# Natural channel order and a 33rd expert pair in a two-layer conv, attention and MoE step

## What is computed

```python
for i in range(2):
    sh1, sc1, g1, sh2, sc2, g2 = split(silu(c) @ ada_w[i] + ada_b[i], 6)   # per stream: c_ctx or c
    h = rms_norm(y, norm_mix[i]) * (1 + sc1) + sh1
    m = conv_module(h) if i == 0 else attention(h)
    y = y + g1 * m
    h = rms_norm(y, norm_ffn[i]) * (1 + sc2) + sh2
    y = y + g2 * (routed_experts(h) + swiglu(h, sh_w_gate[i], sh_w_up[i], sh_w_down[i]))
```

## Time and profile before

| | us |
|---|---|
| median of the 3 executions shown | 1530.44 (1530.39 to 1532.04) |
| the profiled execution's own time | 1527.38 |
| its span, first to last instruction | 1525.6 |
| TensorE busy in it | 1448.5 (95%) |
| VectorE busy | 461.9 (30%) |
| ScalarE busy | 295.8 (19%) |
| HBM traffic | 499.45 MB, mean 327 GB/s |
| mean granted TensorE clock | 0.981 |

### The profile page before, as it was taken

One profiled execution on the slowest core, in us unless ns is written; L12 is line 12 of the kernel. 1 busy time (PEld: TensorE's weight loads), 2 busy tenths in 40 slices (PEclk: granted clock), 3 DMA queues, 4 the chain that ended last, 5 costly groups with the idle time before them and its releaser, 6 DMA issues.

```text
span 1525.6 us, 23849 instructions
## 1 busy us (share of the span) xinstructions
PE 1448.5 (95%) x9543; PEld 846.7 (56%) x9543; DVE 461.9 (30%) x1450; ACT 295.8 (19%) x602; POOL 0.2 (0%) x4
## 2 busy tenths in 40 slices
PE   6899889999999999999979989999999999999995
PEld 2655686555555556555534448755555555555553
DVE  0786543222222222222233522422222222222222
ACT  2300332111111111111121312211111111111111
POOL 0000000000000000000000000000000000000000
PEclk9999989999999999999999999999999999999998
DMA  8988664699999999999941843687999999999980
GB/s 295 331 340 298 256 247 160 256 387 395 401 395 397 406 395 401 407 385 410 407 173 68 325 165 121 279 345 287 393 400 403 400 392 406 398 391 408 401 342 30
DMA packets 87792, 499.45 MB, mean 327 GB/s; under 512 B 11009, under 2 KB 27937, under 8 KB 29888
## 3 DMA queue, kind: packets, MB, share of 16 engines
q1 hardware_dynamic: 87744, 498.79, 82.1%
HBM read 497.45 MB, written 1.31 MB: 327 GB/s over the span
## 4 chain that ended last, share of the span: by engine, by line
PE 90%; DVE 3%; SPq 2%; DMA 2%; ACT 1%; issue 1%; DVEq 0%; ACTq 0%
PE ps L771 30%; PE ps L802 16%; PE ps L752 12%; PE ps L812 8%; PE ps L513 4%; PE ps L488 4%; PE ps L583 3%; PE ps L555 2%; SPq L370 2%; PE ps L708 2%; PE ps L502 1%; DMA S<-in_ada_w_dram 1%; PE ps L790 1%; PE ps L693 1%; PE ps L741 1%; PE ps L564 1%
## 5 line engine op out<-in xcount | busy, mean ns | idle before, releaser
L771 PE MATMUL ps<-ring,W 128*64 128x512 f32 x2048 | 453.4, 594 | 2.1 <-ACT W L1056 2.1
L771 PEld LDWEIGHTS ps<-ring,W 128*64 128x64 f32 x2048 | 165.9, 137 | 282.9 <-issue 277.8
L802 PE MATMUL ps<-ring,W 128*64 128x512 f32 x1024 | 233.8, 598 | 2.1 <-DVE W L1452 2.1
L752 PEld LDWEIGHTS ps<-W,hbf 128*128 128x128 bf16 x3168 | 183.0, 98 | 57.1 <-issue 52.6
L752 PE MATMUL ps<-W,hbf 128*128 128x128 bf16 x3168 | 199.1, 219 | 4.6 <-ACT W L1056 2.2
L1458 DVE TENSOR_TENSOR ypart<-ps,ypart 128x512 fp32r<-128x512 f32 x132 | 91.3, 692 | 192.7 <-ACT ypart L1067 192.7
L812 PE MATMUL ps<-comb,ypart 128*128 128x256 f32 x1056 | 142.5, 287 | 5.7 <-DVE ypart L1458 5.7
L1447 DVE SCALAR_TENSOR_TENSOR W<-W,ps 128x256 f32<-128x256 f32 x66 | 31.7, 480 | 359.4 <-ACT W L1061 359.4
L812 PEld LDWEIGHTS ps<-comb,ypart 128*128 128x128 f32 x1056 | 130.1, 189 | 10.8 <-DVE ypart L1458 9.2
L802 PEld LDWEIGHTS ps<-ring,W 128*64 128x64 f32 x1024 | 67.7, 136 | 118.8 <-issue 109.7
L1056 ACT ACTIVATE W<-ps 128x512 f32<-128x512 f32 x132 | 78.9, 598 | 279.7 <-PE ps L752 279.7
(11 more groups left out here) (195 smaller groups left out, 903.2 us busy)
## 6 DMA issues: line engine op xcount, KB each, us to landing
ring<-in_exp_w_gate_dram SPq DMA_DIRECT2D x128, 1024.0 KB, 8.8
ring<-in_exp_w_up_dram SPq DMA_DIRECT2D x128, 1024.0 KB, 10.8
ring<-in_exp_w_down_dram SPq DMA_DIRECT2D x128, 1024.0 KB, 9.7
S<-in_ada_w_dram SPq DMA_DIRECT2D x48, 1024.0 KB, 7.8
ring<-in_conv_w_dram SPq DMA_DIRECT2D x16, 512.0 KB, 7.3
S<-in_attn_wqkv_dram SPq DMA_DIRECT2D x1, 6144.0 KB, 23.1
ring<-in_conv_w_dram SPq DMA_DIRECT2D x1, 4096.0 KB, 18.3
S<-in_exp_w_gate_dram SPq DMA_DIRECT2D x4, 1024.0 KB, 11.1
```

The lines of the kernel that those rows point to most:

```text
L752: mm = pe.matmul(PG[:, kk * P:(kk + 1) * P], hbf[:, part, g, 4 * half + kk, :], gbf[:, g, :], start=(n == 0), stop=(n == 2 * 3 - 1))
L771: mm = pe.matmul(PGU[64 * b:64 * b + 64, :].rearrange("p (h f) -> p h f", h=2), xg[:, k, 64 * b:64 * b + 64], gate_up_of(w[b])[:, k], star ...
L802: mm = pe.matmul(bank[64 * b:64 * b + 64, :], hidT[:, j, 64 * b:64 * b + 64], down_of(w[b])[:, j, n * 512:(n + 1) * 512], start=(j == 0), ...
```

## The change

It has three parts. (1) Channels are in natural order throughout: chunk k holds channels 128k + p. Every step of eight in a TensorE operand goes; w1, wqkv, wo, the shared weights and the router's are loaded as "(k p) n", with rows of 2 KB, 6 KB, 4 KB, 1 KB (shared down 4 KB) and 256 bytes; w1 in four loads of 2 MB with two semaphores. Since the experts keep their order, the bf16 parts of the input are now put into it by ACT and DVE as they leave PSUM (`by_row`), while `y_parts` and `y_rest` read and write adjacent elements. (2) All small vectors (ada biases, norm gains, conv biases) come as rows of 512 bytes at the start, are transposed by TensorE with the conv taps and copied at once to one tile `vec`; eight loads must be there, not four, before that. `PE_CHUNK` is 3, not 7. (3) The first overflow pair becomes pair 32 of the pipeline, under no condition; its one-hots are built where `one_hot` of the next pair would be.

```diff
-CONV_ORDER = [0, KC - 1] + list(range(1, KC - 1))
-PE_CHUNK = KC - 1
+PE_CHUNK = 3
+CONV_ORDER = [0, PE_CHUNK] + [cc for cc in range(1, KC) if cc != PE_CHUNK]
...
-            return ypart[:, part, :, 64 - 64 * h:128 - 64 * h]
+            return ypart[:, part, 512 - 512 * h:1024 - 512 * h]
-        def by_chunk(bank):
+        def by_row(bank):
             return bank[:, :].rearrange("p (m k) -> p k m", k=KC)
...
+            sp.dma_start(crow[4 * KC:5 * KC, :], conv_b2[0].rearrange("(c p) -> c p", p=P)).then_inc(ld_rows, 16)
+            sp.dma_start(crow[5 * KC:7 * KC, :], norm_mix.rearrange("l (c p) -> (l c) p", p=P)).then_inc(ld_rows, 16)
+            sp.dma_start(crow[7 * KC:9 * KC, :], norm_ffn.rearrange("l (c p) -> (l c) p", p=P)).then_inc(ld_rows, 16)
+            sp.dma_start(arows[0:L * NADA * KC, :], ada_b.rearrange("l (c p) -> (l c) p", p=P)).then_inc(ld_rows, 16)
-            load_ada(range(2))
-            sp.dma_start(adab[:, 0], biases(0)).then_inc(ld_mod0, 16)
-            sp.dma_start(gains[:, 0, 0], cols(norm_mix[0])).then_inc(ld_mod0, 16)
-            sp.dma_start(gains[:, 0, 1], cols(norm_ffn[0])).then_inc(ld_mod0, 16)
-            load_ada(range(2, KC))
-            for cc in CONV_ORDER:
+            load_ada(range(KC))
+            for q in range(2):
                 for h in range(2):
-                    n0 = h * D + cc * P
-                    sp.dma_start(w1[:, :, n0:n0 + P],
-                                 conv_w1[0].rearrange("(p k) n -> p k n", k=KC)[:, :, n0:n0 + P]
-                                 ).then_inc(ld_w1[cc], 16)
+                    n0 = h * D + q * 512
+                    sp.dma_start(w1[:, :, n0:n0 + 512],
+                                 conv_w1[0].rearrange("(k p) n -> p k n", p=P)[:, :, n0:n0 + 512]
+                                 ).then_inc(ld_w1[q], 16)
...
                     for j in range(4):
-                        rhs = ada[:, slot, (j // 2) * D:(j // 2 + 1) * D].rearrange(
-                            "p (m q) -> p q m", q=KC)[:, 4 * (j % 2):4 * (j % 2) + 4, :]
-                        mm = pe.matmul(bank[32 * j:32 * j + 32, :].rearrange("p (q m) -> p q m", q=4),
-                                       scT[:, k, :], rhs, start=(k == 0), stop=(k == KC - 1))
+                        mm = pe.matmul(bank[32 * j:32 * j + 32, :], scT[:, k, :], ada[:, slot, j * 512:(j + 1) * 512],
+                                       start=(k == 0), stop=(k == KC - 1))
...
-                                           w[:, k, :].rearrange("p (m q) -> p q m", q=KC)[:, 2 * b + h, :],
+                                           w[:, k, (2 * b + h) * P:(2 * b + h + 1) * P],
...
-                pair(PAIRS - 1, 1, 0, N_LOOP + 2, last=True)
-                combine(PAIRS - 1, 1)
+                pair(PAIRS - 1, 1, 0, N_LOOP + 2)
+                pair(PAIRS, 0, 1, N_LOOP + 2, last=True)
+                combine(PAIRS, 0)
...
-                with pe.If(nov > 0):
-                    overflow_pair(0, 0)
-                    with pe.If(nov > 2):
-                        overflow_pair(0, 1)
+                with pe.If(nov > 2):
+                    overflow_pair(0, 1)
...
-                    act.activation(dst, ps[i][:, :], ACT.Copy).then_inc(ht_b1, 1)
+                    act.activation(hbf[:, 0, g, :, 64 * h:64 * h + 64], by_row(ps[i]), ACT.Copy).then_inc(ht_b1, 1)
...
-                        act.activation(half_of(0, h), by_chunk(bank), ACT.Copy).then_inc(act_yhi[l], 1)
+                        act.activation(half_of(0, h), bank[:, :], ACT.Copy).then_inc(act_yhi[l], 1)
...
+            dve.tensor_copy(vec[:, :], ps[7][:, 0:V_W]).then_inc(rows_in, 1)
...
+                def pair(i, par, last=False, overflow_next=False):
+                    if overflow_next:
+                        overflow_hot(PAIRS, 0)
+                    elif not last:
                         one_hot(i + 1)
...
-                pair(PAIRS - 1, 1, last=True)
+                pair(PAIRS - 1, 1, overflow_next=True)
+                pair(PAIRS, 0, last=True)
```

More of the change, by code:

```diff
@@ L204, in build_kernel @@
         crow = W[:, 3584:3712]
+        arows = W[:, 3712:3840]
         hb_f = hbf[:, :, :, :, :].rearrange("p s g k m -> p (s g k m)").bitcast(F32)
@@ L458, in overflow_pair @@
                         load_expert_at(l, e[b], 2 * (1 - half) + b, "dn")
-                with sp.If(nov > 0):
-                    overflow_pair(0, 0)
-                    with sp.If(nov > 2):
-                        overflow_pair(0, 1)
-                        with sp.If(nov > 4):
-                            with sp.Fori(1, OVF_PAIRS // 2) as it:
-                                for half in range(2):
-                                    with sp.If(nov > 4 * it + 2 * half):
-                                        overflow_pair(it, half)
+                overflow_pair(0, 0)
+                with sp.If(nov > 2):
+                    overflow_pair(0, 1)
+                    with sp.If(nov > 4):
+                        with sp.Fori(1, OVF_PAIRS // 2) as it:
+                            for half in range(2):
+                                with sp.If(nov > 4 * it + 2 * half):
+                                    overflow_pair(it, half)
                 if l == 0:
                     sp.wait_ge(pe_dn[0], 6)
-                    sp.dma_start(wqkv, attn_wqkv[0].rearrange("(p k) n -> p k n", k=KC)).then_inc(ld_qkv, 16)
+                    sp.dma_start(wqkv, attn_wqkv[0].rearrange("(k p) n -> p k n", p=P)).then_inc(ld_qkv, 16)
             for g, y in enumerate((y_prompt, y_sample)):
@@ L811, in combine @@
                         for part in range(2):
-                            pe.matmul(acc[k // 2][:, (k % 2) * TT:(k % 2 + 1) * TT], ypart[:, part, k, :],
+                            pe.matmul(acc[k // 2][:, (k % 2) * TT:(k % 2 + 1) * TT], ypart[:, part, k * P:(k + 1) * P],
                                       comb[:, par, :], start=False, stop=False, skip_group_check=True)
@@ L956, in _ @@
                         ada_copy(e, ps[e % 3])
-                    squares(dwo, 2, cv_out, lambda k: k + 1)
+                    squares(dwo, 2, cv_out, lambda k: k + 1 if k < PE_CHUNK else k)
                     for cc in range(KC):
@@ L1047, in _ @@
                     act.wait_ge(ht_r1, 4 * l + i + 1)
-                    dst = hbf[:, 1, g, 4 * h:4 * h + 4, :].rearrange("p k m -> p (k m)")
-                    act.activation(dst, ps[i][:, :], ACT.Copy).then_inc(ht_b2, 1)
+                    act.activation(hbf[:, 1, g, :, 64 * h:64 * h + 64], by_row(ps[i]), ACT.Copy).then_inc(ht_b2, 1)
                 act.wait_ge(sh_gu, l + 1)
@@ L1084, in _ @@
                         pair(2 * it + half + 3)
-                pair(PAIRS - 1, last=True)
+                pair(PAIRS - 1)
+                pair(PAIRS, last=True)
                 def overflow_pair(it, par):
@@ L1457, in y_rest, with overflow_hot @@
                         dve.wait_ge(act_yhi[l], 2 * i + 1 + h)
-                        dve.tensor_tensor(half_of(1, h), by_chunk(bank), half_of(0, h), ALU.subtract
+                        dve.tensor_tensor(half_of(1, h), bank[:, :], half_of(0, h), ALU.subtract
                                           ).then_inc(dve_ylo[l], 1)
-                def pair(i, par, last=False):
-                    if not last:
+                def overflow_hot(i, j):
+                    e = [dve.value_load(table[0:1, bass.ds(2 * j + b + 1, 1)], min_val=0, max_val=NE - 1)
+                         for b in range(2)]
+                    dve.wait_ge(dve_ov[l], 3 * j + 1)
+                    for b in range(2):
+                        dve.tensor_copy(wst[:, :, :, b:b + 1], wt3[:, :, :, bass.ds(e[b], 1)])
+                        for g in range(G):
+                            ins = dve.tensor_scalar(gbf[:, g, 64 * b:64 * b + 64], iota,
+                                                    ovrank[:, g, bass.ds(e[b], 1)], None, ALU.is_equal)
+                        if b == 0:
+                            ins.then_inc(dve_ov[l], 1)
+                            dve.wait_ge(dve_ov[l], 3 * j + 2)
+                        else:
+                            ins.then_inc(dve_g[l], 1)
+                            dve.wait_ge(dve_g[l], i + 1)
+                        dve.tensor_scalar(ovrank[:, :, :], ovrank[:, :, :], -float(SLOTS), None, ALU.add
+                                          ).then_inc(dve_ov[l], 1)
+                        dve.wait_ge(dve_ov[l], 3 * j + b + 3)
+                def pair(i, par, last=False, overflow_next=False):
+                    if overflow_next:
+                        overflow_hot(PAIRS, 0)
+                    elif not last:
                         one_hot(i + 1)
```

136 lines of the change are left out of this document (52 added, 84 removed).

## The result

| | before | after |
|---|---|---|
| median of the executions timed side by side, 4 each | 1530.41 us (1530.03 to 1532.04) | 1518.12 us (1517.27 to 1519.93) |
| the profiled execution's own time | 1527.38 | 1518.69 |
| its span | 1525.6 | 1516.9 |
| mean granted TensorE clock | 0.981 | 0.948 |

The ratio is 0.9923, with a 95% interval of 0.9911 to 0.9934: faster by 12.3 us, not by the 42.8 that I forecast. 1518.1 lies above the whole range. The change did most of what it was to do, and then TensorE ran at half its clock through most of the heads of layer 1's attention.

The account below looks back on a forecast made before the run. TensorE was taken to bound the expert loop, which the change leaves alone; gains lie at loop ends and mixers: 10.3 + 16.5 + 7.8 + 4.8 + 1.7 + 0.8 + 0.9 = 42.8 off 1530.44, giving 1487.6 us, range 1481 to 1514.

Parts of the forecast that it names:

- part 2: Ada products: adjacent columns save 0.875 us a unit; 17.1 in the conv stage, 7.8 in layer 1's attention.
- Part 3: Conv stage start: first product waits for half of w1, at 44 against 43.4 us; loss 0.6, bounds gain 2, loss 4.
- what is late next is DVE: Conv stage: DVE's last chunk could start at 133.3 instead of 153.05 us, allowing TensorE savings up to 19.8.
- The last square: Conv stage end: the last DVE chunk is squared last, so one square and its sum fewer, 0.8 us saved.
- rival B: Ada unit halves but w1's half, DVE's chain or the one-hots come late: 5 to 9 less saved, 1493 to 1497; chance 0.1.
- The tails: Expert loops' ends: the overflow pair inside the pipeline takes 30.68 instead of 35.86 us; 5.2 saved per layer, 10.3 in both.
- The halving of an ada unit: Ada products: a unit of 8 records falls from 1.87 to 1.0 us; saving 0.9, bounds 0 and 1.0.
- rival A: Ada unit stays at 1.87 us, four streams sharing what one step wasted: 18.4 saved, 1512 us; chance 0.22.
- The stationary operand: Weights no longer loaded in steps: 2.4 us saved in each of two projections, 4.8 together, and 1.7 in shared down.
- Output copies with the end: Kernel's end: four output copies go from 1121 towards 597 ns but wait for transposes; 0.9 us saved, bounds 0.5 and 2.
- Rival C: Overflow pair gains nothing, its weights late in the pipeline: 10.3 less saved, 1498 us; chance 0.03.
- Rival D: Natural-order loads of w1 and wqkv run far below their rate, at 100 GB/s: 39 us slower, 1570; chance 0.03.

Follow-up runs that it names:

- zeros ahead of the heads: Changed kernel with zero-operand products added after each of the four ada units ahead of layer 1's attention heads (32 to 35): 1493.89 us, ratio 0.9772.
- quarters: Changed kernel with w1 loaded in four column quarters (eight 1 MB loads, 1 KB rows) and TensorE's chunk put at 1: 1514.93 us, ratio 0.9905.
- quarters and zeros together: Changed kernel with w1 in four column quarters and zero-operand products after the four ada units ahead of the heads: 1492.62 us, ratio 0.9752.
- zeros between the heads: Changed kernel with zero-operand products only after ada units 36 to 39, one in each of the first four heads: 1500.28 us, ratio 0.9813.

## Why the prediction was wrong, and where it was right

**The step that failed** is in part 2, *attention of layer 1*: "10 x 0.875 = 8.75; DVE and ACT between heads would show about 1 of it: 7.8". It counted units at the full clock and took for granted that the rest of the stage kept the clock it had. None of the rivals was this: the prediction took the clock of every stage as given, though the stage table shows it for each. In its place the runs show a loss of 22.1: the clock costs 24.3 (143.75 against 119.5 with zeros ahead of the heads), and what remains beside it is a gain of 2.1, not 7.8. In that run the part from the first head on took 59.69 instead of the 63.51 of before, 3.8 less: the ten units took 12.0 instead of 19.6, and lower clock toward the end, in two stretches between 860 and 881, gave half of that back (its line 660, which is line 642 of the changed kernel, took 3.61 there for sixteen records and 1.93 at the full clock). From the gain of 3.8 goes 1.7 for the qkv product, 36.27 instead of 34.57; its first 10 us ran at a clock of 0.83, where the kernel before had 1.00.

How the fall comes about shows in the timeline of TensorE after, ahead of the heads:

```profile
816.93 1.94 PE L482 MATMUL ps<-S,scT 128*32 128x512 f32 x8 [2.79 <-DMA S<-in_ada_w_dram]
...
825.12 1.07 PE L482 MATMUL ps<-S,scT 128*32 128x512 f32 x8 [1.35 <-DMA S<-in_ada_w_dram]
```

TensorE has four units to do there and waits for DVE's normalisation and for each unit's transfer. Before, a unit ran 2.02, with waits of 0.4 to 1.3 between; the clock was low for 3 us, from about 835, and came back. After, the same transfers feed units with half the work. The first three ran at the low clock and so took 1.94, 1.93 and 1.86; the clock was low from 817, came back between 823 and 824 and fell again at 827, behind a stretch from 823 to 827 in which TensorE was busy for 1.84 of 4 us. After that TensorE was busy for 32.79 of 34 us at the low level and was not granted the high one: a busy stage in the profile is no sign that it has its clock. Every remedy that was tried also moved the moments at which the clock fell and rose, so the runs show that the missing work lowered it, and not by which rule.

So the work taken away ahead of the heads lay under waits, where it was worth nothing, and its price came just behind, where nothing waits for transfers. The Trainium skill (TensorE: Matmul & The Clock Gate, HAM oscillation — how this bites in real kernels) tells of a loop that loses its clock again and again because each stretch of products is shorter than the wait for the next transfer. The rows ahead of the heads agree in part: the clock falls there, 0.66 with 7.07 of 11 us busy, though only two of the four waits, 2.79 and 1.35, are longer than the unit behind them (1.94 and 1.07). The Trainium skill (the same page, What's actually happening) also has the clock at its full level after sustained work, and there the measurement decides otherwise: 0.50 with 32.79 of 34 us busy.

**Part 3** was mis-sized. "44 against 43.4" measured 47.07 (bound: a loss of 4; 3.65 lost). The term is "I take 32" for the end of the eight ada units. The timeline of TensorE after has the last of them, whose wait for its transfer ends at 36.31:

```profile
36.31 1.06 PE L482 MATMUL ps<-S,scT 128*32 128x512 f32 x8 [1.53 <-DMA S<-in_ada_w_dram]
```

With the 10.8 for half of w1 that gives 47.1. The wait for that half is 8.22, and quarters take it away. And "what is late next is DVE ... that allows 19.8" put DVE's chain at an uninterrupted pace from the gate of its fourth chunk (94.10 before, 97.21 after). It was interrupted: with the 31-tap product and four units on TensorE ahead of the product for DVE's fifth chunk, DVE idles 4.48 and its last gate comes at 114.82 + 2 x 13.05, measured 140.93. TensorE was ready for it at 129.31 + 7.17 + 0.6 = 137.1. So: TensorE saved 19.6 past its start (17.1 forecast; a unit saved 0.98 and not 0.875), less 3.65 for the start, less 3.8 for DVE: 12.1 and not 16.5. The last square, of which I forecast 0.8, gave 0.3. That is rival B's mechanism, two of its three cases at once, at 4.4 instead of 5 to 9.

**Right, with sizes.** The tails: 5.30 and 5.23 measured for 5.15 each, and 11.1 when undone; the last pair took 14.98 to the hundredth, and the one-hots stayed hidden (`hidden` of pair 31 waited 3.39 for ACT, where it had waited 5.96). The halving of an ada unit, the uncertain term: 0.89 for a unit where the prediction had 1.0, so four groups with adjacent columns lose next to nothing beside each other; rival A falls. (Its sum left in the 0.5 that its sentence takes out: 17.9 saved, and 1512.5.) The Trainium skill (Advanced Engine Details and Errata, Memory Cachelines) names a penalty where each access meets another 16-byte line, not its size; the trace agrees that there is one, and makes it about a doubling: 1096 ns in steps, a median of 593 without; a unit 1.87 and 0.89. The stationary operand: the projections gained 2.16 and about 3.0, for 2.4 each; 30.8 fell to 27.8. Shared down 0.82 for 0.85. Output copies with the end 1.26 for 0.9; a copy fell from 1121 to 597 ns. Rival C fell with the tails.

**Rival D** (natural-order loads far below their rate) had nothing in it. The queues moved 383 to 400 GB/s between 28 and 60, while w1 came in with rows of 2 KB. Page of the profile after, transfers with the us from issue to landing:

```profile
ring<-in_conv_w_dram SPq DMA_DIRECT2D x4, 2048.0 KB, 19.0
S<-in_attn_wqkv_dram SPq DMA_DIRECT2D x1, 6144.0 KB, 25.4
```

wqkv was issued at 724.63, so it was there by 750.0, 17.8 before its product at 767.85. The Trainium skill (DMA: Bandwidth & Descriptors, Latency and other measured facts) has 103 GB/s for partitions 4 MiB apart; no run here has that pitch. With a partition's pieces of w1 1 MB apart the queues kept the 383 to 400 above.

Left open: which quantity of TensorE's work the clock follows, and whether its amount or its moment decides; why the clock ahead of the attention was lower with quarters and zeros together; and how the stretches at 0.5 near the end of the attention could be filled without delaying the loads.

## What to carry to other kernels

Before costing work off TensorE at what it saves, look at the granted clock of the stage it leaves and of the next one: where TensorE waits for transfers or for another engine, a shorter product leaves the wait as it is and can halve the speed of everything behind it. The test is cheap: put the removed work back as products with zeros; if the time falls and the granted clock rises, it was the clock, and the zeros under the wait are themselves a remedy. And when one large load replaces many small ones, cost the first product by all the bytes ahead of it: here those of the units before it were the ones mis-sized.

## What the runs showed of the hardware

- A shorter product can make a kernel slower: in steps the 16 units of the attention take 1.95 us each at the full clock, adjacent 0.99, and with the longer ones the kernel was 19.3 us faster (1498.83 against 1518.12).
- At 0.5 of its clock TensorE stayed for 65 us (827 to 892) though it was busy for 32.79 of the 34 us from 828 on; in the run with zeros between the heads, 7.27 of 8 us busy, it was back after 7 us.
- Zeros after the first two of the four units ahead of the heads gain nothing, after all four everything: 1518.15 and 1493.89.
- Moving-operand columns 32 bytes apart nearly double a float32 record (593 to 1096 ns), with or without steps in the PSUM that it writes; stationary columns 32 bytes apart cost about a tenth (27.8 to 30.8 us for 128).
- Four column groups of 32 output partitions, with adjacent columns, run eight records in 0.89 us, 0.44 for a round of four, which is what line 766 takes for a round of two groups of 64 (453.3 us for 1024 rounds).
